# Three query/key chunks of each first-block layer multiplied as raw fp32 instead of as a split pair

## What is computed

```python
z = h @ w_in + b_in
q, k, v, glu_in, gates = jnp.split(z, [...], axis=-1)
q = apply_rope(rmsnorm(q.reshape(shp), q_norm[:, None, :]), cos, sin)
k = apply_rope(rmsnorm(k.reshape(shp), k_norm[:, None, :]), cos, sin)
...
u = a * jax.nn.sigmoid(g)
u = conv(u, 31 taps, depthwise) + conv_b; layer norm; silu
...
return (g_attn * y_attn + g_conv * y_conv) @ w_out
```

## Time and profile before

| | us |
|---|---|
| median of 3 runs | 2137.08 (2129.70 to 2138.32) |
| the profiled execution, device time | 2135.44 |
| its span, first to last instruction | 2133.7 |
| PE busy | 1999.0 (94%) |
| DVE busy | 1541.7 (72%) |
| ACT busy | 1047.1 (49%) |
| bytes read | 335 MB, 158 GB/s over the span |

### The profile page before, as it was taken

How to read it: one execution, slowest core, us unless ns; L and a number is a source line. 1 busy time by engine, 2 the same in 40 slices (tenths; PEclk the granted TensorE clock), 3 DMA queues, 4 the chain that set the end, 5 groups by cost and what they waited for, 6 DMA issues and landing times.

```text
span 2133.7 us, 39079 instructions
## 1 busy us (share of the span) xinstructions
PE 1999.0 (94%) x15904; PEld 1908.7 (89%) x15904; DVE 1541.7 (72%) x2190; ACT 1047.1 (49%) x1368; POOL 0.2 (0%) x4
## 2 busy tenths in 40 slices
PE   7999998999999899999989999996989997988998
PEld 7999997888999899999968899995788997778998
DVE  6556899987755665588999666555657775657777
ACT  5445454564444444454536554442455554455554
POOL 0000000000000000000000000000000000000000
PEclk9999999999999999999999999998999998999999
DMA  6555555125555355655522455542235553215554
GB/s 244 188 186 207 204 195 179 65 64 193 198 187 186 139 197 177 219 194 192 178 105 70 128 197 199 187 168 73 80 115 182 182 196 119 90 43 197 194 185 150
DMA packets 56698, 344.31 MB, mean 161 GB/s; under 512 B 7440, under 2 KB 7440, under 8 KB 20496
## 3 DMA queue, kind: packets, MB, share of 16 engines
q1 hardware_dynamic: 55584, 340.29, 45.9%
q10 hardware_dynamic: 1008, 2.51, 0.3%
HBM read 335.43 MB, written 1.05 MB: 158 GB/s over the span
## 4 chain that ended last, share of the span: by engine, by line
PE 67%; DVE 23%; ACT 6%; DMA 3%; issue 2%; ACTq 0%; DVEq 0%; SPq 0%
PE bank L421 21%; PE bank L422 21%; PE bank L423 21%; DVE lo L1407 7%; DVE cv L1643 5%; ACT hi L934 3%; DMA raw<-in_w 2%; PE bank L467 1%; DVE qn L1566 1%; DVE p_sb L1622 1%; DVE qk L1593 1%; PE bank L612 1%; DMA x<-in_x 1%; DVE sq L1437 0%; DVE x L1474 0%
## 5 line engine op out<-in xcount | busy, mean ns | idle before, releaser
L1407 DVE TENSOR_TENSOR lo<-raw,hi 128x2048 fp32r<-128x2048 f32 (+1 forms) x342 | 716.2, 2095 | 266.9 <-ACT hi L934 266.6
L934 ACT ACTIVATE hi<-raw 128x2048 fp32r<-128x2048 f32 (+1 forms) x342 | 598.1, 1753 | 108.4 <-PE bank L423 77.1
L421 PE MATMUL bank<-n_hi,hi 128*128 128x256 f32 x2112 | 595.1, 282 | 37.3 <-DVE n_lo L1411 14.8
L422 PE MATMUL bank<-n_lo,hi 128*128 128x256 f32 x2112 | 592.4, 280 | 0.0
L423 PE MATMUL bank<-n_hi,lo 128*128 128x256 f32 x2112 | 592.2, 280 | 0.0
L421 PEld LDWEIGHTS bank<-n_hi,hi 128*128 128x128 f32 x2112 | 403.6, 191 | 40.1 <-DVE lo L1670 12.5
L423 PEld LDWEIGHTS bank<-n_hi,lo 128*128 128x128 f32 x2112 | 400.4, 190 | 0.0
L421 PE MATMUL bank<-h_hi,hi 128*128 128x256 f32 x1296 | 382.1, 295 | 19.2 <-DVE h_lo L1411 17.2
L422 PEld LDWEIGHTS bank<-n_lo,hi 128*128 128x128 f32 x2112 | 399.1, 189 | 0.2
L422 PE MATMUL bank<-h_lo,hi 128*128 128x256 f32 x1296 | 371.0, 286 | 0.0
L423 PE MATMUL bank<-h_hi,lo 128*128 128x256 f32 x1296 | 370.3, 286 | 0.0
(11 more groups left out here) (231 smaller groups left out, 2296.5 us busy)
## 6 DMA issues: line engine op xcount, KB each, us to landing
raw<-in_w SPq DMA_DIRECT2D x281, 1024.0 KB, 4.9
raw<-in_w SPq DMA_DIRECT2D x64, 512.0 KB, 3.8
zr<-zg SPq DMA_DIRECT2D x96, 64.0 KB, 3.0
bv<-in_bv SPq DMA_DIRECT2D x2, 768.0 KB, 6.2
spread<-in_spread SPq DMA_DIRECT2D x2, 768.0 KB, 8.5
x<-in_x ACTq DMA_DIRECT2D x4, 256.0 KB, 10.2
mask_in<-in_const SPq DMA_DIRECT2D x2, 512.0 KB, 7.1
out_x<-x SPq DMA_DIRECT2D x1, 1024.0 KB, 3.9
```

The source lines that it names most:

```text
L421: mm(out, w_hi, a_hi, start=start, stop=False, skip_group_check=True)
L422: mm(out, w_hi, a_lo, start=False, stop=False, skip_group_check=True)
L934: fn(hi[:, s, 0:w], raw[:, s, 0:w], ACT.Copy).then_inc(sem["hi"], 1)
L1407: v.tensor_tensor(lo[:, s, 0:w], raw[:, s, 0:w], hi[:, s, 0:w].bitcast(F32), ALU.subtract)\
```

## The change

Chunks 3, 6 and 9 of the twelve are called plain. For these there is no `hi` and no `lo`: ACT and DVE skip their `split`, and PE multiplies each of the 16 tiles once, the raw fp32 weights by the fp32 input in `sq`, as soon as the load has landed. All three chunks use slot 0 (as do chunks 0 and 12). Since nobody makes `lo` of a plain chunk, the load of the next chunk of its slot (6, 9 and 12) waits for PE's end of the plain chunk instead. Nothing else is moved.

```diff
+PLAIN = (QK0 + 3, QK0 + 6, QK0 + 9)
+def plain_1(c):
+    return c in PLAIN
...
-        def chunk(c, src, half):
-            sp.wait_ge(sem["lo"], cnt.up("lo"))
+        def chunk(c, src, half, plain=False):
+            if plain:
+                sp.wait_ge(sem["pe"], first["pe"] + (c - SLOTS) + 1)
+            else:
+                sp.wait_ge(sem["lo"], cnt.up("lo"))
...
             for c in range(VA0, FFN2_0):
-                chunk(c, d["w1"][l * CHUNKS1 + c], half_chunk_1(c))
+                chunk(c, d["w1"][l * CHUNKS1 + c], half_chunk_1(c), plain_1(c - SLOTS))
                 i = c - QK0 - 5
                 if 0 <= i < 2 * QK_CHUNKS:
                     turn_halves(i)
...
+        def plain_pairs(c, out):
+            pe.wait_ge(load[c % SLOTS], first[f"load{c % SLOTS}"] + 16 * (c // SLOTS + 1))
+            for k in range(KT):
+                for j in range(2):
+                    last = mm(out[:, j * S:(j + 1) * S], tile(raw, c, 2 * k + j), sq[:, k, :], start=(k + j == 0),
+                              stop=(k == KT - 1), skip_group_check=True)
+            last.then_inc(sem["pe"], 1)
...
-                pairs(c, bank[c % 3], 0, KT, h_hi, h_lo, True)
+                if plain_1(c):
+                    plain_pairs(c, bank[c % 3])
+                else:
+                    pairs(c, bank[c % 3], 0, KT, h_hi, h_lo, True)
                 qk_tail1(i)
...
-                split(QK0 + i + 2)
+                split(QK0 + i + 2, plain=plain_1(QK0 + i + 2))
                 qk_step1(i)
...
-                split(QK0 + i + 2)
+                split(QK0 + i + 2, plain=plain_1(QK0 + i + 2))
                 qk_at(i)
```

More of the change, by code:

```diff
@@ L192, with _stream @@
 PER_FFN2 = dict(_FFN_LOOP, tap0=2, conv3=2, link=2)
-def _stream(chunks):
-    return dict(hi=chunks, lo=chunks, pe=chunks, slot=chunks, load0=16 * chunks // 3,
+def _stream(chunks, plain=0):
+    return dict(hi=chunks - plain, lo=chunks - plain, pe=chunks, slot=chunks, load0=16 * chunks // 3,
                 load1=16 * chunks // 3, load2=16 * chunks // 3)
@@ L205 @@
 PER_LAYER1 = dict(
-    _stream(CHUNKS1), **_ffns(2), x=16, sq=16, stat=4, std=4, h32=16, hhi=16, h=16, prm=1,
+    _stream(CHUNKS1, len(PLAIN)), **_ffns(2), x=16, sq=16, stat=4, std=4, h32=16, hhi=16, h=16, prm=1,
     bv=48, mask=1, sig=8, u=8, z=12, qstat=12, qstd=2, qrstd=2, qbc=12, zg=12, turn0=6 * 64, turn1=6 * 64, rope=12, qk=12, bg=1, v=3, gate=8,
@@ L344, in sp_program @@
     def sp_program(sp):
-        cnt = Count({})
-        def chunk(c, src, half):
-            sp.wait_ge(sem["lo"], cnt.up("lo"))
+        cnt = Count(dict(pe=SLOTS))
+        first = {}
+        def chunk(c, src, half, plain=False):
[3 more added lines that the diff above has]
+                sp.wait_ge(sem["lo"], cnt.up("lo"))
             w = CW // 2 if half else CW
@@ L385, in sp_program @@
             layer = cnt.begin()
+            first["pe"] = cnt.at("pe")
             if l == 0:
@@ L399, in sp_program @@
             ffn_stream(l, d["w1"], FFN2_0, CHUNKS1)
-            cnt.end(layer, dict(lo=CHUNKS1, zg=2 * QK_CHUNKS, rope=2 * QK_CHUNKS))
+            cnt.end(layer, dict(lo=CHUNKS1 - len(PLAIN), pe=CHUNKS1, zg=2 * QK_CHUNKS, rope=2 * QK_CHUNKS))
         for l in range(L):
@@ L721, in layer1 @@
             first["qk"] = cnt.at("qk")
+            for s in range(SLOTS):
+                first[f"load{s}"] = cnt.at(f"load{s}")
             ffn(0, PER_FFN1, True, by_halves=l == 0)
@@ L926, in take, with split @@
             act.wait_ge(sem[name], cnt.up(name, k))
-        def split(c, half=False):
+        def split(c, half=False, plain=False):
             s = c % SLOTS
             w = CW // 2 if half else CW
+            if plain:
+                cnt.up(f"load{s}", 16)
+                cnt.up("slot")
+                return
             act.wait_ge(load[s], cnt.up(f"load{s}", 16))
```

## The result

The changed kernel takes **2156.69 us** (median of 4 runs, 2151.16 to 2162.23) against 2135.32 before (4 runs, 2129.70 to 2138.32). The ratio is 1.0103, with a 95% interval of 1.0069 to 1.0138: slower by 15 to 29 us. The forecast was 2151 us in a range of 2140 to 2162.

A forecast was written before the change was run, and what follows sets the result against it. PE decides on average, DVE near the stage's end. PE's 3.5 and 0.2 us, then 6.0 us for the copies, start DVE 7.6 us late per layer; 2 x 7.6 = 15.2 on 2135.4, said as 2151 us, range 2140 to 2162.

The forecast's parts named there:

- PE's price: Plain chunks on PE: 16 fp32 matmuls of 0.433 us, 1.17 us more per chunk, 3.5 us per layer by chunk 9's end.
- The new wait on SP's queue: Loads of chunks 6, 9 and 12 wait for PE's end of the plain chunk, holding up the `turn_halves` copies behind them.
- The three DVE waits: DVE waits for the copies in rounds 3, 6 and 9: nearly 8, 3 and 3 us per layer.
- from PE's end until the last copy has landed: SP wakes, issues the load and four copies, the last lands: 6.0 us, bounds 4.35 and 6.85.
- the last landing: Part of the copies' delay: the fourth copy lands 3.4 us after its issue, with a load just ahead.
- PE's end of chunk 9: PE ends the third plain chunk 3.5 us later, plus 0.2 for a late reciprocal: 342.2 instead of 338.51.
- the low bound: Shortest delay from PE's end to the last copy, 4.35 us, using the shortest landing of all copies, 2.0 us.
- The third place: DVE's `rope1(7)` in round 9: copies land at 348.2, DVE starts 7.6 us late and works on without removed work.
- PE's wait before the scores: PE's idle time before its first score matmul (L667) grows from 10.4 to about 14 us.
- The first rival: Copies are not late: PE's 3.5 us against DVE's 6.6 leaves +0.2 us per layer, 2136 to 2137; chance 14%.
- the loads themselves have time: Late loads on SP's queue: PE needs the slot's next chunk some 13 us later, a load lands in 5.4 us.
- The savings: Three skipped `lo` save DVE 6.6 us per layer in rounds 1, 4 and 7, but only shorten waits there anyway.

The follow-up runs named there:

- Experiment 2: The changed kernel with the loads of chunks 6, 9 and 12 issued by ACT's queue instead of SP's; 1.0043 of the kernel before, +9.2 us.
- experiment 4: The changed kernel with chunks 3, 6 and 9 loaded by ACT into the unused `lo` slot, no load waiting for PE on SP; 1.0011 of the kernel before.
- experiment 3: The changed kernel with `hi` and `lo` of the plain chunks still made but unread, PE and SP waiting for these `lo`; 1.0126 of the kernel before.
- experiment 1: The kernel before, all chunks split, with only the loads of chunks 6, 9 and 12 waiting for PE on SP's queue; ratio 1.0103, +22.0 us.
- experiment 6: The changed kernel with only chunk 3 plain; 1.0070 of the kernel before, +14.9 us.
- experiment 7: The changed kernel with only chunk 9 plain; 1.0058 of the kernel before, +12.4 us.

## Why the prediction was right, and where it was short

**PE's price.** Right: 7.17 us for 16 fp32 matmuls, start to start 7.10, against 5.93; with the start-up taken off (0.17 us, as in the split chunk) that is 0.433 us each and 1.17 more per chunk, as read from two places at full clock. In experiments 2 and 4 PE ends chunk 9 just 3.5 us later than before, as forecast. The rule of four passes in the Trainium skill ("FP8 and Floating Point Precision", TensorE Precision Notes) gives no time for a pass. At a split step's 0.12 us each, as the prediction took them, a matmul would be 0.48 us and a chunk 7.7 to 7.9, which the trace doesn't show; four passes of 0.108 us would fit it. Without the late copies DVE's saving covers this price (experiment 4). With them it does count: it stands in the sum with 3.5 us, and experiment 3 has a stage 2.2 us longer than experiment 1. Experiment 1 comes to the same loss without it, since PE there waits 3.3 us for the reciprocal and runs at a low clock behind that wait, and the last copy lands later.

**The new wait on SP's queue.** Right, and it is the cause: experiment 1 makes the loss with it alone, and experiments 2 and 4 take it away and lose 9 and 2 us. The three DVE waits came as named: nearly 8, 3 and 3 us forecast, 8.7, 3.1 and 3.5 measured.

**Its size was short twice.** These are the two terms of the sum that were too small. The step "from PE's end until the last copy has landed" was put at 6.0 us and measured 6.65 to 6.98. Its term for the last landing was taken as 3.4 us from a place where the copies had been issued 0.9 us behind the load; here they go out 0.4 us behind it and take 4.3 us (those behind the load of 343.77). And PE's end of chunk 9 was put 3.7 us later (three times 1.17 and 0.2); it was 343.67 - 338.51 - 0.60 = 4.6 us later, since PE's wait for the late reciprocal is 1.0 us and not 0.2. The sum by the measured terms is 4.6 + 6.7 - 2.1 = 9.2 us per layer, the trace has 9.15 in layer 0. Twice 7.6 was 15 us; the traces' stages give 19, the two measurements 20 and 22. So 2151 was about 6 us too low, inside the range. At none of the three places did the last copy land before the load ahead of it (5.4 to 5.9 us after its issue, the copies 6.65 and more after PE's end), so the 4.35 us kept as the low bound was not seen; this agrees with the order within a ring that the Trainium skill states ("DMA: Bandwidth & Descriptors", Queues, rings and completion order).

**The third place decides.** Right in the changed kernel, and experiments 6 and 7 show the general form: each place alone costs about 6 us, all three cost 9.

**PE's wait before the scores** was put at 14 us and is 12.4: PE was itself late by its new waits at L608 (2.3 and 1.0 us), which the walk had counted only in part.

**The first rival was priced wrongly.** It said that with the copies in time nothing would be lost. Experiment 2 has the copies in time and loses 9.2 us. The working let the `hi` of chunk 12 follow PE's end of chunk 9 by 3.67 us, as if its data were there; but the same change lets its load start only at PE's end, and 5.5 us of load stand in between. The prediction had said that "the loads themselves have time", which holds for a plain chunk, needed by PE two rounds later, and not for chunk 12, which must be split first. Only with the data in a place of its own (experiment 4) is the rival's zero reached.

**The savings.** Only in part right. The prediction let the three skipped `lo` shorten nothing but waits that were there anyway. Experiment 3 shows that in the changed kernel 4.1 of the 6.6 us count: with the three `lo` kept the reciprocal comes later, PE waits longer for it and runs at a low clock behind this wait, and the third place moves. The forecast didn't suffer, since its walk had these `lo` skipped and the reciprocal nearly in time. With a place of their own for the plain chunks nothing is gained in the end, since DVE then waits 1.13 us for the `hi` of chunk 12, which comes 3.5 us later for PE's fp32 products (experiment 4).

## What to carry to other kernels

When a buffer is no longer released by the early reader but by the late one, look first at what is queued behind the wait for it: here four copies of 64 KB behind one load cost more than three chunks of slower matmuls (22 us in experiment 1 against 2 in experiment 4). Then count again when the next user of the buffer gets its data, since an early release was also its prefetch. And a saving on an engine is worth something only behind its last wait for the others, or where another engine waits for it in turn: two `lo` skipped in the last rounds gained 6.6 us, three skipped earlier, against dearer products on PE, nothing once the loads were in time (experiment 4), but 4.1 us a stage where PE waited for DVE's reciprocal (experiment 3).

## What the runs showed that was not expected

A short PE wait in the middle of the stage could cost more than its own length, since a stretch at a low granted clock followed it. Both layers of these traces taken together, the lowest clock of any 2 us behind such a wait was:

| PE's wait before L608 or its counterpart | where | granted clock |
|---|---|---|
| 3.0 to 3.9 us | seven, in experiments 1, 3 and 6 | 0.50 to 0.52 |
| 1.7 to 1.9 us | two in experiment 7, one in layer 1 of the changed kernel | 0.50 |
| 1.85 us | one, in layer 1 of the changed kernel's second trace | 1.00 |
| 0.9 to 1.6 us | nine, in both traces of the changed kernel and in experiments 1 and 3 | 1.00 |

Two executions of one kernel differ here at 1.85 and 1.88 us, so the length of the wait alone does not decide. The longest stretch is in experiment 6: behind a wait of 3.0 us the clock stays at 0.50 until 341 us, and from the end of the wait to the end of chunk 9, a split chunk there, it is 9.06 us instead of 6.56. The Trainium skill ("TensorE: Matmul & The Clock Gate", Why this matters for your kernels) advises against idle gaps between bursts of matmuls; the waits of 3.0 us and more agree with it, and those of 1.7 to 1.9 us show that shorter gaps could do it too.

Copies in the shadow of large loads varied. The last copy of a group landed 3.4 us after its issue at the place read in the kernel before, where the next 1 MB load went out 5.75 us behind the first; it was 4.3 to 4.7 us at the three places of the changed kernel and 6.2 us at the third place of experiment 1, and at all four two more loads went out within some 6 us of the first. Why it took 6.2 us there was not tried.
